# RWKV-7 time mix in a two-block network, one Trainium2 core: the next head pair's inputs one step later in VectorE's order and in smaller pieces, the inverse's first level ahead of the values' product, two result matrices behind that level

## The chip, the cores and the metric

The kernel runs on one core of one Trainium2 chip. The metric is the device time of one execution in microseconds (us). Three executions of the kernel before the change took 4197.87, 4207.27 and 4209.8 us; their median is 4207.27.

## What is computed

Two transformer-like blocks of two layers each, on a sequence of 512 positions with width 1024, all in float32. The change touches only one part of the second block's layers, the RWKV-7 time mix, which therefore runs twice in an execution. Cut to what matters, for 8 heads of 64 channels:

```python
z = z + (z_prev - z) * mu                    # token shift, per channel
r, k, v, lw, la, lg = split(z)
decay = exp(-exp(-0.5) * sigmoid(w0 + tanh(lw) @ w_up))
a = sigmoid(a0 + la @ a_up);  g = sigmoid(lg) @ g_up
kk = k * k_k;  kk = kk * rsqrt(max(sum(kk * kk), 1e-24))   # per head
kf = k * (1 + (a - 1) * k_a)
def step(state, r_t, w_t, k_t, v_t, ka_t, kb_t):           # ka = -kk, kb = kk * a
    sa = state @ ka_t
    state = state * w_t + outer(sa, kb_t) + outer(v_t, k_t)
    return state, state @ r_t
y = scan(step)                               # over 512 positions
yn = (y - mean) * rsqrt(var + eps) * ln_w + ln_b
out = (yn + sum(r * kf * r_k) * v) * g
```

## The kernel before

**The chunked form.** The recurrence isn't walked position by position. The 512 positions are cut into 8 chunks of 64. Within a chunk, products of 64x64 matrices (called grams here) of the decayed tensors `at`, `bt`, `kt`, `rt` give AT (the matrix to be inverted) and TM (its transpose), AK, RB and RK. The inverse of the triangular matrix is built by five doubling levels (`lv` 1 to 5). Each level is a product X on TensorE, its eviction to XS by ScalarE, a product T on TensorE, and the addition of T into the inverse (`T2`, `TTM`) by VectorE. W1 is the product of AK and the values. After the levels come MN (the inverse times `at` and W1), DP and E (the chunk's state update), a chain of six small products S1 to S6 (the state through the chunks, each step TensorE then VectorE), and the outputs Y and YS.

**Pairs.** Heads are taken two at a time, four pairs `pp` = 0 to 3 in each of the two time mixes. For each pair, `back(pp)` is the chunk algebra above, and `front(pp)` makes the pair's inputs: the projections k, r and v (each 24 matmuls of 512 columns in four quarters, line 2556), the decay, the normalised key, and from them `at`, `bt`, `kt`; and the bonus and gate (`bon`, `g`). The product `sq` (line 2578) sums the key's squares within a head, `bon` (line 2587) sums r*kf*r_k.

**The order.** Every engine runs its own instruction list in program order. In each list the function `interleaved` runs `front(0)` alone, and then alternates, one step at a time, `back(pp)` and `front(pp + 1)`; a step is what stands between two `yield`s. So the place of a `yield` decides behind which piece of `back` a piece of the next pair's `front` stands. Beside `back(3)` TensorE does matmuls of the following gate stage (line 3029) in place of a front. An instruction whose data aren't there yet holds up all that stands behind it on its engine.

**Engines of the pieces.** On VectorE: line 2802 adds the shifted token (for k, r, v), 2812 and 2816 are the decay's scan, 2830 is kf, 2833 evicts `sq`, 2836 is kk, 2841 is `at`, 2842 and 2845 make `bt`, 2848 is the factor for `bon`, 2849 is `kt`, 2857 and 2859 finish bonus and gate. Of back, 2864 masks the grams, 2870 and 2874 make the inverse's start, 2872 is `rt`, 2888 adds T of levels 1 to 4, 2891 that of level 5, 2894 evicts half of MN, 2899, 2902 and 2905 take DP and E, 2910 is a step of the state's chain. `vector_finish` (2515 to 2526) is the normalisation of the pair before. On GpSimd: 2930 squares the key, 2941 and 2943 prepare the levels' masks (`OFF`, one instruction a level), and `gpsimd_feed` (1481) splits a 128x1024 half of the weights into a high and a low part, after `scalar_feed` (ScalarE, 1467) has made the high part. On ScalarE: 2709 evicts a projection, 2745 and 2747 are the logarithm and exponential that make the inverse root of `sq`, 2777 evicts X.

**PSUM.** Banks 6 and 7 belong to front. Banks 0 to 5 go round for back's products in the order of the list `BACK`; a product waits until the earlier user of its bank has been evicted.

## Time and profile before

| | us |
|---|---|
| median of three executions | 4207.27 |
| lowest, highest | 4197.87, 4209.8 |
| the profiled execution, its time | 4199.9 |
| the profiled execution, its span | 4198.1 |
| first time mix, from the first gram of pair 0 (2165.3) to YS of pair 3 (2423.8) | 258.5 |
| distance between the first grams of pairs 1 and 2 | 66.2 |

The span is the time between the first and last instruction that the trace shows; the execution's own time is 1.8 us more. TensorE is busy for 94% of the span. The work of the two time mixes is alike: each has four pairs of some 64 to 66 us, with its own prologue (front of pair 0) ahead.

### The profile page before, as it was taken

What the parts mean: (1) busy time and instruction counts of PE and PEld (TensorE: products, weight loads), DVE (VectorE), ACT (ScalarE), POOL (GpSimd) and SP (SyncE); (2) the same over time, 40 slices, a digit from 0 to 9 for tenths busy, and PEclk for the clock granted to TensorE, in tenths of its full rate; (3) what the DMA queues carried; (4) which work ended last, traced back from release to release, by engine and by line L of the source; (5) the groups of instructions that cost most, each with busy time, mean ns of one, the idle gap of its engine ahead of it and who ended that gap; (6) DMA issues with size and microseconds to landing.
All of it is one profiled execution on the core that took longest, in us unless ns stands there. A gap on an engine that the chain in (4) does not pass through costs nothing.

```text
span 4198.1 us, 60801 instructions
## 1 busy us (share of the span) xinstructions
PE 3932.4 (94%) x25980; PEld 3121.3 (74%) x25980; DVE 1771.6 (42%) x2671; ACT 1435.1 (34%) x2275; POOL 1190.3 (28%) x725
## 2 busy tenths in 40 slices
PE   7988899999989899999988899999999889999998
PEld 6966678888777678877666787788776667877886
DVE  3266232323254633435845422334368454224333
ACT  3256222222244633332432333333324332333332
POOL 2010122222211033332332235333323322353332
PEclk9999999999999999999999999999999999999999
DMA  5014133323111022222111022222211100222221
GB/s 206 31 58 151 51 116 106 111 93 101 67 61 43 31 83 96 100 71 76 51 36 37 22 86 95 83 99 97 85 66 51 41 27 32 91 90 82 99 94 67
DMA packets 61358, 323.55 MB, mean 77 GB/s; under 512 B 6177, under 2 KB 6305, under 8 KB 36257
## 3 DMA queue, kind: packets, MB, share of 16 engines
q1 hardware_dynamic: 61088, 319.65, 22.1%
q8 instruction: 207, 3.39, 0.3%
q14 instruction: 63, 0.51, 0.0%
HBM read 317.53 MB, written 2.10 MB: 76 GB/s over the span
## 4 chain that ended last, share of the span: by engine, by line
PE 80%; DVE 6%; issue 5%; ACT 3%; POOL 3%; DMA 2%; SPq 0%; DVEq 0%; POOLq 0%; ACTq 0%
PE ps L1509 50%; PE ps L704 3%; PE ps L724 3%; PE ps L2556 3%; PE ps L1521 2%; PE ps L338 2%; PE ps L2192 1%; DMA adab<-in_wada 1%; PE ps L3029 1%; PE ps L1008 1%; PE ps L1043 1%; PE ps L2635 1%; PE ps L1023 1%; PE ps L2180 1%; PE ps L2648 1%
## 5 line engine op out<-in xcount | busy, mean ns | idle before, releaser
L1883 DVE SCALAR_TENSOR_TENSOR ftmp<-ps,vec,ftmp 128x511 f32<-128x511 f32 (+2 forms) x440 | 301.6, 694 | 357.4 <-ACT ftmp L1837 236.2
L1481 POOL TENSOR_TENSOR PWL<-ring,PWH 128x1024 fp32r<-128x1024 f32 (+2 forms) x116 | 266.7, 2299 | 609.6 <-ACT PWH L1467 609.6
L1481 POOL TENSOR_TENSOR WL<-ring,WH 128x1024 fp32r<-128x1024 f32 (+3 forms) x102 | 227.0, 2226 | 618.4 <-ACT WH L1467 601.9
L1467 ACT ACTIVATE PWH<-ring 128x1024 fp32r<-128x1024 f32 (+2 forms) x216 | 211.8, 982 | 480.3 <-PE ps L1509 446.1
L1467 ACT ACTIVATE WH<-ring 128x1024 fp32r<-128x1024 f32 (+3 forms) x160 | 158.7, 993 | 627.4 <-PE ps L1509 590.7
L1509 PE MATMUL ps<-FH,WH 128*128 128x512 f32 x1008 | 311.4, 363 | 0.0
L1509 PE MATMUL ps<-FH,WL 128*128 128x512 f32 x1008 | 305.6, 358 | 0.0
L1509 PE MATMUL ps<-FL,WH 128*128 128x512 f32 x1008 | 304.3, 356 | 0.0
L1481 POOL TENSOR_TENSOR PW3L<-ring,PW3H 128x1024 fp32r<-128x1024 f32 (+2 forms) x92 | 210.5, 2288 | 278.1 <-ACT PW3H L1467 277.8
L1474 DVE TENSOR_TENSOR PWL<-ring,PWH 128x1024 fp32r<-128x1024 f32 (+2 forms) x100 | 125.5, 1257 | 357.4 <-ACT PWH L1467 357.4
L1509 PEld LDWEIGHTS ps<-FH,WH 128*128 128x128 f32 x1008 | 167.8, 190 | 37.2 <-issue 9.1
L1906 POOL TENSOR_TENSOR ftmp<-ftmp 128x512 f32<-128x512 f32 (+1 forms) x88 | 126.0, 1432 | 231.9 <-DVE ftmp L1883 231.7
L1509 PEld LDWEIGHTS ps<-FL,WH 128*128 128x128 f32 x1008 | 167.4, 189 | 29.8
L1509 PEld LDWEIGHTS ps<-FH,WL 128*128 128x128 f32 x1008 | 167.1, 189 | 29.8
L1467 ACT ACTIVATE PW3H<-ring 128x1024 fp32r<-128x1024 f32 (+2 forms) x106 | 104.2, 983 | 248.4 <-PE ps L1509 237.1
L1509 PE MATMUL ps<-FH,PWL 128*128 128x512 f32 x432 | 170.9, 396 | 0.0
L1509 PE MATMUL ps<-FL,PWH 128*128 128x512 f32 x432 | 170.5, 395 | 0.0
L1509 PE MATMUL ps<-AH,WH 128*128 128x512 f32 (+1 forms) x528 | 164.5, 366 | 6.2 <-DVE AL L1888 6.2
L1509 PE MATMUL ps<-FH,PWH 128*128 128x512 f32 x432 | 169.6, 393 | 0.0
L1474 DVE TENSOR_TENSOR WL<-ring,WH 128x1024 fp32r<-128x1024 f32 (+3 forms) x58 | 67.1, 1157 | 235.2 <-ACT WH L1467 235.1
L1509 PE MATMUL ps<-AH,WL 128*128 128x512 f32 (+1 forms) x528 | 160.4, 358 | 0.0
L1509 PE MATMUL ps<-AL,WH 128*128 128x512 f32 (+1 forms) x528 | 159.6, 357 | 0.0
(599 smaller groups left out, 9805.8 us busy)
## 6 DMA issues: line engine op xcount, KB each, us to landing
ring<-in_wup SPq DMA_DIRECT2D x88, 1024.0 KB, 4.8
adab<-in_wada SPq DMA_DIRECT2D x56, 512.0 KB, 5.5
ring<-in_wgate SPq DMA_DIRECT2D x24, 1024.0 KB, 4.9
ring<-in_wdown SPq DMA_DIRECT2D x24, 896.0 KB, 4.7
ring<-in_win SPq DMA_DIRECT2D x18, 1024.0 KB, 4.8
ring<-in_wout SPq DMA_DIRECT2D x16, 1024.0 KB, 4.9
ring<-in_wada SPq DMA_DIRECT2D x14, 1024.0 KB, 5.2
ring<-in_wdown SPq DMA_DIRECT2D x12, 1024.0 KB, 5.0
```

The costliest lines, as they stand in the source:

```text
L338: e.matmul(bank(6 + i)[:, 0:n], C("ones"), buf(k * len(segs) + i)[:, 0:n], start=k == 0, stop=k == 7).then_inc(*sum_mm.up(tag, k, i))
L704: mm = e.matmul(pr[:, c:c + n], ww[:, k, :], h[part][:, k, :], start=k == 0 and x == 0, stop=k == 7 and x == 2)
L724: mm = e.matmul(out, x, ww[:, k, :], start=kk == 0 and n == 0, stop=kk == 7 and n == 2)
L1008: mm = e.matmul(two(a)[:, n:n + d_ - c], PF[r, BASE[kq] + jt, qc:qc + 128], PF[r, BASE[kk] + jt, c:d_], start=True, stop=True)
L1467: e.activation(wh, view, ACT.Copy).then_inc(*whi_a.up(L, n))
L1474: e.tensor_tensor(wl, view, wh.bitcast(F32), SUB).then_inc(*wlo_v.up(L, n))
L1481: e.tensor_tensor(wl, view, wh.bitcast(F32), SUB).then_inc(*wlo_g.up(L, n))
L1509: mm = e.matmul(out[:, c:c + h.shape[1]], ww[:, k, :], h, start=at == 0 and p == 0, stop=at == K - 1 and p == 2)
L1521: mm = e.matmul(outs[j][:, c:c + h.shape[1]], ww[:, k, :], h, start=k == order[0] and ww is ws[j][0] and part == 0, stop=k == order[-1] an ...
L1883: e.scalar_tensor_tensor(out=dst, in0=src, scalar=conv_cols(L, ch, a), in1=dst, op0=MUL, op1=ADD).then_inc(*(ffn_v.up(L, "tap", x, j, c) i ...
L1906: e.tensor_tensor(zg, zg, zv, MUL).then_inc(*ffn_g.up(L, x))
L2556: mm = e.matmul(front_bank(what), ww[:, k, :], h, start=k == 0 and x == 0, stop=k == 7 and x == 2)
```

## The change

It does four things; all are moves, and no arithmetic instruction is added or removed.

- On VectorE all of the next pair's front stands one step later or more, so behind the levels' additions where it stood ahead of them: the decay's scan behind T1's addition, K behind T3's, and, above all, R, kk, `at`, `bt` behind T5's. The piece that held R, kk, `at` and `bt` is cut into R; kk and `at`; and bon's factor with `bt`. ScalarE's order is fitted to it (R is evicted ahead of the logarithm).
- On TensorE the products `sq`, `bon` and `g` come one step or more later.
- At the head of back, X of level 1 comes ahead of W1, and the grams RB and RK move from ahead of them to behind T of level 1, with their masks on VectorE. `rt` is made after AK's mask. The order of PSUM banks follows.
- On GpSimd the k weights' split comes ahead of the squares of the key.

```diff
-        BACK = ([... for x in ("AT", "TM", "tok0", "tok1", "tok2", "tok3", "AK", "RB", "RK", "W1")] ...
+        BACK = ([("AT", 2), ("TM", 2)] + [(f"tok{i}", 1) for i in range(4)] + [("AK", 2)] + level(1, "X") + [("W1", 1), ("mean", 1)] + level(1, "T")
+                + [("RB", 2), ("RK", 2)] + level(2, "X") + [("var", 1)] + level(2, "T") + [y for lv in range(3, 6) for x in "XT" for y in level(lv, x)]
...
 tensor front
                     quarter(q, pp, "r")
-                    if q == 1:
+                    if q == 2:
                         w.wait_ge(rw_v.at(L, pp, "K"), rw_g.at(L, pp, "sq"))
                         e.matmul(front_bank("sq"), ...)
...
                     quarter(q, pp, "v")
-                    if q == 2:
-                        w.wait_ge(rw_v.at(L, pp, "R"), rw_v.at(L, pp, "bon"))
-                        e.matmul(front_bank("bon"), ...)
                     if q < 3:
                         yield 1
+                yield 1
+                w.wait_ge(rw_v.at(L, pp, "R"), rw_v.at(L, pp, "bon"))
+                e.matmul(front_bank("bon"), ...)
                 yield 1
                 w.wait_ge(rw_v.at(L, pp, "V"), rw_a.at(L, "sig"))
                 e.matmul(front_bank("g"), ...)
...
 tensor back
                 gram("AK", kt, at, kt_)
-                gram("RB", bt, rt, rt_)
-                gram("RK", kt, rt)
                 yield 1
-                (the W1 product)
                 for lv in range(1, 6):
                     (the X product of both halves)
+                    if lv == 1:
+                        (the W1 product)
                     next(fin, None)
                     yield 1
                     (the T product of both halves)
+                    if lv == 1:
+                        gram("RB", bt, rt, rt_)
+                        gram("RK", kt, rt)
                     yield 1
...
 vector front
+                yield 1
                 w.wait_ge(rw_a.at(L, pp, "lw"))
                 (scan, lp, u, K, KN, kf)
                 yield 1
+                yield 1
                 w.wait_ge(rw_mm.at(L, pp, "sq"))
                 e.tensor_scalar(TSQ, front_bank("sq"), ...)
                 yield 1
+                shifted((L, pp, "R"), R, front_bank("r"), pp)
+                yield 1
                 w.wait_ge(rw_a.at(L, pp, "isq"))
                 e.tensor_tensor(KN, KN, TSQ, MUL)
-                yield 1
-                shifted((L, pp, "R"), R, front_bank("r"), pp)
                 (at)
+                yield 1
+                (bon's factor)
                 (b, bt)
                 yield 1
-                (bon's factor)
                 e.tensor_tensor(kt, KF, TGI, MUL)
-                yield 1
-                yield 1
                 yield 1
                 shifted((L, pp, "V"), VV, front_bank("v"), 8 + pp)
                 yield 1
                 (bonus)
+                yield 1
                 (gate)
...
 vector back
-                w.wait_ge(rw_a.at(L, pp, "GT"))
-                e.tensor_tensor(rt, R, GT, MUL)
                 mine(L, pp, "TTM0")
                 e.tensor_tensor(TTM, TTM, many("id2"), ADD)
                 masked("AK", AKT, "su")
-                masked("RB", RBT, "iu")
-                masked("RK", RKT, "iu")
+                w.wait_ge(rw_a.at(L, pp, "GT"))
+                e.tensor_tensor(rt, R, GT, MUL)
...
                     (T additions of level lv)
+                    if lv == 1:
+                        masked("RB", RBT, "iu")
+                        masked("RK", RKT, "iu")
...
 gpsimd front
+                gpsimd_feed(e, w, F, pair_view(pp + 1, "k"))
                 w.wait_ge(rw_v.at(L, pp, "KN"), ...)
                 e.tensor_tensor(TSQ, KN, KN, MUL)
-                gpsimd_feed(e, w, F, pair_view(pp + 1, "k"))
```

In the diff, what stands in brackets or as "..." within a line is unchanged code told in a word. All tensors of this part are cells of one tile `ar`; so the rows that follow are told apart by their lines.

VectorE before, from T4's additions (2888) of pair 1 to the masks of DP: kk (2836), R (2802), `at` (2841), `bt` (2842, 2845), and only then T5's additions (2891), bon's factor (2848), `kt` (2849), MN's eviction (2894).

```order
L2888 TENSOR_TENSOR ar<-ar,ps 128x2x256 x2
L2836 TENSOR_TENSOR ar<-ar,HC 128x512
L2802 SCALAR_TENSOR_TENSOR ar<-ps,vec,ar 128x511
L2841 SCALAR_TENSOR_TENSOR ar<-ar,HC 128x512
L2842 TENSOR_TENSOR ar<-ar 128x512
L2845 TENSOR_TENSOR ar<-ar,HC 128x512
L2891 TENSOR_TENSOR ar<-ar,ps 128x256 x2
L2848 SCALAR_TENSOR_TENSOR ar<-ar,vec 128x512
L2849 TENSOR_TENSOR ar<-ar,HC 128x512
L2894 COPY ar<-ps 128x4x2x64
L2899 TENSOR_TENSOR ar<-ps,cst 128x512
```

The same place on VectorE after the change (its own line numbers: 2892 is T4, 2839 the eviction of `sq`, 2895 T5, 2806 R, 2901 MN, 2844 kk, 2847 `at`, 2906, 2909 and 2912 DP and E, 2850 bon's factor, 2851 and 2854 `bt`).

```order
L2839 TENSOR_SCALAR HC<-ps 128x512
L2895 TENSOR_TENSOR ar<-ar,ps 128x256 x2
L2806 SCALAR_TENSOR_TENSOR ar<-ps,vec,ar 128x511
L2901 COPY ar<-ps 128x4x2x64
L2844 TENSOR_TENSOR ar<-ar,HC 128x512
L2847 SCALAR_TENSOR_TENSOR ar<-ar,HC 128x512
L2906 TENSOR_TENSOR ar<-ps,cst 128x512
L2909 TENSOR_TENSOR ar<-ps,ar 128x512
L2912 TENSOR_TENSOR ar<-ar,ps 128x512
L2850 SCALAR_TENSOR_TENSOR ar<-ar,vec 128x512
L2851 TENSOR_TENSOR ar<-ar 128x512
L2854 TENSOR_TENSOR ar<-ar,HC 128x512
```

What stood ahead of T5's additions stands behind them; kk and `at` now lie between MN's eviction and DP's, and bon's factor and `bt` ahead of the first step of the state's chain (2917), which is the next row.

TensorE before, at the head of pair 1: AT and TM (the first 2605), the transposes, AK with RB and RK (the second 2605, 48 matmuls), W1 (2625), X1 (2635), the mean of the pair before.

```order
L2605 MATMUL ps<-ar 64x64 x32
L2615 MATMUL ps<-cst,ar 128x128 x16
L2605 MATMUL ps<-ar 64x64 x48
L2625 MATMUL ps<-ar 64x64 x16
L2635 MATMUL ps<-ar 64x64 x16
L2494 MATMUL ps<-XC,cst 128x512
```

The same place after the change: the second group of grams (2606) is AK alone, 2628 is X1, 2636 is W1.

```order
L2606 MATMUL ps<-ar 64x64 x32
L2616 MATMUL ps<-cst,ar 128x128 x16
L2606 MATMUL ps<-ar 64x64 x16
L2628 MATMUL ps<-ar 64x64 x16
L2636 MATMUL ps<-ar 64x64 x16
L2495 MATMUL ps<-XC,cst 128x512
```

The 32 matmuls of RB and RK stand behind T1 now, ahead of the first quarter of the next k.

## Rows read from the trace of the kernel before

**Rows 1.** The page's first part: span, and busy time of each engine.

```profile
span 4198.1 us, 60801 instructions
...
PE 3932.4 (94%) x25980; PEld 3121.3 (74%) x25980; DVE 1771.6 (42%) x2671; ACT 1435.1 (34%) x2275; POOL 1190.3 (28%) x725
```

**Rows 2.** Waits of TensorE, first time mix (2130 to 2460): us, times, longest.

```profile
PE ps L2658 <- DVE ar L2891: 11.1, 3, 3.7
```

**Rows 3.** The same view of the second time mix (3280 to 3600).

```profile
PE ps L2658 <- DVE ar L2891: 11.2, 3, 3.7
```

**Rows 4.** The same view of pair 1, its first row left out.

```profile
PE ps L2682 <- DVE ar L2910: 1.5, 3, 0.7
PE ps L2592 <- DVE ar L2802: 1.3, 1, 1.3
PE ps L2625 <- DVE ar L2864: 1.0, 1, 1.0
PE ps L2635 <- DVE ar L2888: 1.0, 1, 1.0
PE ps L2605 <- DVE ar L2872: 0.6, 1, 0.6
PE ps L2556 <- ACT HC L2727: 0.4, 1, 0.4
```

**Rows 5.** Timeline of VectorE in pair 1: start, duration, instruction, idle before.

```profile
2258.40 2.89 DVE L2830 TENSOR_TENSOR ar<-ar,XC 128x512 f32<-128x512 f32 x1
...
2270.68 2.84 DVE L2842 TENSOR_TENSOR ar<-ar 128x512 f32<-128x512 f32 x1
...
2274.16 0.75 DVE L2891 TENSOR_TENSOR ar<-ar,ps 128x256 f32<-128x256 f32 x2
2274.83 0.75 DVE L2848 SCALAR_TENSOR_TENSOR ar<-ar,vec 128x512 f32<-128x512 f32 x1
...
2278.56 0.69 DVE L2894 COPY ar<-ps 128x512 f32<-128x512 f32 x1 [2.39 <-PE ps L2658]
...
2284.99 0.28 DVE L2910 SCALAR_TENSOR_TENSOR ar<-ps,ar 128x64 f32<-128x64 f32 x1 [1.45 <-PE ps L2682]
```

**Rows 6.** Timeline of GpSimd in pair 1.

```profile
2258.37 2.37 POOL L1481 TENSOR_TENSOR PWL<-ring,PWH 128x1024 fp32r<-128x1024 f32 x1
2270.41 2.56 POOL L1481 TENSOR_TENSOR PW3L<-ring,PW3H 128x1024 fp32r<-128x1024 f32 x1 [9.67 <-ACT PW3H L1467]
```

**Rows 7.** Timeline of TensorE: MN to Y's start, pair 1, then MN, pair 3.

```profile
2275.06 3.47 PE L2658 MATMUL ps<-ar 64*64 64x128 f32 x32 [3.71 <-DVE ar L2891]
2278.45 0.50 PE L2556 MATMUL ps<-PXH,PWH 128*128 128x512 f32 x1
...
2291.81 0.49 PE L2691 MATMUL ps<-ar 64*64 64x64 f32 x7
...
2403.38 1.96 PE L2658 MATMUL ps<-ar 64*64 64x128 f32 x32
2405.28 0.51 PE L3029 MATMUL ps<-PXH,PWH 128*128 128x512 f32 x1
```

**Rows 8.** Busy times over pair 1's MN; 0.60 is TensorE's granted clock.

```profile
2275.00:2279.00 4.00, 3.94 (x34) 3.74 (x35) 1.61 (x3) 0.44 (x1) 0.00 (x0) 0.60 0.55 229
```

**Rows 9.** Timeline of VectorE, head of pair 1: masks of AK, RB, RK.

```profile
2235.37 1.87 DVE L2864 TENSOR_TENSOR ar<-ps,cst 128x512 f32<-128x512 f32 x3
```

**Rows 10.** Line 2943 in 2229 to 2242: nanoseconds of one, least, median and most.

```profile
L2943 POOL TENSOR_TENSOR ar<-ar,cst x5: 1271/1286/1742, 2233.2 to 2239.0; 128x512 f32<-128x512 f32 x5
```

**Rows 11.** Timeline of TensorE: W1 in pair 1, then W1 in pair 2.

```profile
2236.10 1.15 PE L2625 MATMUL ps<-ar 64*64 64x64 f32 x32 [1.04 <-DVE ar L2864]
...
2301.88 1.84 PE L2625 MATMUL ps<-ar 64*64 64x64 f32 x32 [1.04 <-DVE ar L2864]
```

**Rows 12.** Timeline of TensorE in the first prologue: `sq` and `bon`.

```profile
2148.22 1.10 PE L2578 MATMUL ps<-HC,cst 128*128 128x512 f32 x2 [0.93 <-POOL HC L2930]
...
2158.53 1.88 PE L2587 MATMUL ps<-ar,cst 128*128 128x512 f32 x2 [2.30 <-DVE ar L2848]
```

More of the change, by code:

```diff
@@ L2432, in program, with level @@
         FRONT_BANK = {"w": 6, "a": 7, "k": 6, "r": 7, "sq": 6, "bon": 7, "v": 6, "g": 6}
-        BACK = ([(x, 1 if x[0:3] == "tok" or x == "W1" else 2) for x in ("AT", "TM", "tok0", "tok1", "tok2", "tok3", "AK", "RB", "RK", "W1")]
-                + [((x, lv, h), 1) for lv in range(1, 6) for x in ("X", "T") for h in range(2)]
+        def level(lv, x):
+            return [((x, lv, h), 1) for h in range(2)]
+        BACK = ([("AT", 2), ("TM", 2)] + [(f"tok{i}", 1) for i in range(4)] + [("AK", 2)] + level(1, "X") + [("W1", 1), ("mean", 1)] + level(1, "T")
+                + [("RB", 2), ("RK", 2)] + level(2, "X") + [("var", 1)] + level(2, "T") + [y for lv in range(3, 6) for x in "XT" for y in level(lv, x)]
                 + [("MN", 2), ("DP", 2), ("E", 2)] + [(("S", c), 1) for c in range(1, 7)] + [("Y", 2), ("YS", 1)])
-        at_lv = BACK.index((("X", 1, 1), 1)) + 1
-        BACK = BACK[:at_lv] + [("mean", 1)] + BACK[at_lv:at_lv + 4] + [("var", 1)] + BACK[at_lv + 4:]
         def back_banks():
@@ L2584, in front @@
                     quarter(q, pp, "v")
-                    if q == 2:
-                        w.wait_ge(rw_v.at(L, pp, "R"), rw_v.at(L, pp, "bon"))
-                        e.matmul(front_bank("bon"), C("b64"), BON[pp % 2], start=True, stop=True).then_inc(*rw_mm.up(L, pp, "bon"))
                     if q < 3:
                         yield 1
+                yield 1
+                w.wait_ge(rw_v.at(L, pp, "R"), rw_v.at(L, pp, "bon"))
+                e.matmul(front_bank("bon"), C("b64"), BON[pp % 2], start=True, stop=True).then_inc(*rw_mm.up(L, pp, "bon"))
                 yield 1
@@ L2617, in back @@
                 gram("AK", kt, at, kt_)
-                gram("RB", bt, rt, rt_)
-                gram("RK", kt, rt)
                 yield 1
-                pr = back_ps("W1")
-                w.wait_ge(*back_free(L, pp, "W1"), rw_v.at(L, pp, "AK"), rw_a.at(L, pp, "tok3"))
-                for t, hh, s in UNITS:
-                    z = 2 * t + hh
-                    mm = e.matmul(pr[rows(s), z * 64:z * 64 + 64], AKT[rows(s), z, :], vtk[rows(s), z, :], start=True, stop=True)
-                mm.then_inc(*rw_mm.up(L, pp, "W1"))
                 fin = tensor_finish(e, w, L, pp - 1) if pp else iter(())
@@ L2637, in back @@
                         mm.then_inc(*rw_mm.up(L, pp, "X", lv, h))
+                    if lv == 1:
+                        pr = back_ps("W1")
+                        w.wait_ge(*back_free(L, pp, "W1"), rw_v.at(L, pp, "AK"), rw_a.at(L, pp, "tok3"))
+                        for t, hh, s in UNITS:
+                            z = 2 * t + hh
+                            mm = e.matmul(pr[rows(s), z * 64:z * 64 + 64], AKT[rows(s), z, :], vtk[rows(s), z, :], start=True, stop=True)
+                        mm.then_inc(*rw_mm.up(L, pp, "W1"))
                     next(fin, None)
@@ L2841, in front @@
                 e.scalar_tensor_tensor(out=at, in0=KN, scalar=-1.0, in1=TLP, op0=MUL, op1=MUL).then_inc(*rw_v.up(L, pp, "at"))
+                yield 1
+                mine(L, pp, "R")
+                e.scalar_tensor_tensor(out=BON[pp % 2], in0=R, scalar=vc("rw_r_k_2", 4 * l + pp), in1=KF, op0=MUL, op1=MUL).then_inc(*rw_v.up(L, pp, "bon"))
                 e.tensor_tensor(bt, KN, AA, MUL).then_inc(*rw_v.up(L, pp, "b"))
@@ L2846, in front @@
                 yield 1
-                mine(L, pp, "R")
-                e.scalar_tensor_tensor(out=BON[pp % 2], in0=R, scalar=vc("rw_r_k_2", 4 * l + pp), in1=KF, op0=MUL, op1=MUL).then_inc(*rw_v.up(L, pp, "bon"))
                 e.tensor_tensor(kt, KF, TGI, MUL).then_inc(*rw_v.up(L, pp, "kt"))
-                yield 1
-                yield 1
                 yield 1
```

16 lines of the change are left out of this document (9 added, 7 removed).

## The prediction

> **What bounds the kernel now.** The page comes first: TensorE is busy for 3932.4 of 4198.1 us [rows 1], so only what makes TensorE wait, or work slowly, can move the time, and all four edits lie inside the two time mixes. The next view is therefore who TensorE waits for there. One cause stands far above the rest: MN (2658) waits for T5's additions (2891), three times 3.7 us in each mix, 11.1 and 11.2 us [rows 2, 3]. It is three times and not four because pair 3 has no front beside it. The same view of one pair lists what else is left: 1.3 us ahead of `g`, 1.5 us in the state's chain, 1.0 ahead of W1, 1.0 ahead of X2, 0.6 ahead of RB, 0.4 ahead of k [rows 4]; with MN's 3.7, some 9.5 of a pair's 66.2 us.
>
> Why are T5's additions late? VectorE's timeline answers. `bt`'s first product (2842) stands ahead of them and takes 2.84 us [rows 5], where other instructions of its size take 0.69 [rows 5]. It starts 0.27 us after GpSimd's split of weights, 2270.41 to 2272.97 [rows 6], and ends 0.55 us after it, so it stood still until GpSimd was through. T5's additions start at 2274.16 and TensorE goes on at 2275.06, having stood since 2271.35 [rows 5, 7].
>
> The wait has a second price. MN's 32 matmuls take 3.47 us behind the wait and 1.96 in pair 3, where none is [rows 7]; the granted clock over them is 0.60 [rows 8], so that part of the time ran at the lower level, 1.2 GHz. From MN's start to that of the next matmul it is 3.39 against 1.90 us [rows 7]: 1.49 us a pair.
>
> The Trainium skill ("SBUF — State Buffer", Who interferes with whom) says that a VectorE instruction with two SBUF inputs contends with a GpSimd instruction that reads SBUF, the later one waiting the other out. By that rule, the trace agrees (2.84 against 0.69 us).
>
> **The parts and their costs.** I walk each pair in the new order with the durations of the old trace.
>
> *T5 first.* In the new order only the eviction of `sq`, a 0.69 us instruction whose product is done a step earlier, stands between T4's and T5's additions. T5's products end about when the first quarter of v starts, so the two additions (0.75 us together) are over before that quarter (1.7 us) is. MN's wait goes: 3.71 x 3 = 11.1 us a mix. With no wait the clock has no cause to fall there: 1.49 x 3 = 4.5 us. Bounds for the clock: nothing (it falls anyway) to 1.49.
>
> *The late stretch on VectorE.* What left T5's front goes where TensorE is in MN to S6. From MN's end VectorE must do: N 0.69, kk and `at` 1.4, DT, E and P 2.1, bon's factor and `bt` 2.1, S1 0.28, `kt` 0.7, S2, V 0.75, S3, bonus 0.7, S4, gate 0.7, S5, S6: 11 us, of which each large one costs about 0.7 and each step of the chain 0.28 [rows 5]. TensorE took 13.4 us from the quarter behind MN, 2278.45, to Y, 2291.81 [rows 7], 2.8 of them in waits [rows 4], so it has 10.6 us of work there and the two are nearly level. Walking it: E is evicted 4.5 us after MN's end, P, bon's factor and `bt` last until 7.0, S1's eviction until 7.3, so S2 waits 0.3 us; bon fills S3's wait and `g` finds V just ready; S5 waits 0.5 (behind the gate's eviction), S6 0.6. Sum 1.4 us, against 1.3 + 1.5 = 2.8 before [rows 4]: a gain of 1.4 x 3 = 4.3 us a mix. This is where the change adds waits: bon's factor and `bt` now have S1's eviction and with it the chain queued behind them, and kk (which waits for ScalarE's root, now behind R's eviction and a 1.05 us split) has DT, E and P behind it. ScalarE is done some 1.7 us before kk's turn. GpSimd's split of the r weights ended at 2272.97 [rows 6]; 1.4 us sooner (the head's gain, below) that is 2271.6. MN can start at 2271.35 less 1.4, ends 1.96 later and N takes 0.69 [rows 5, 7], so kk starts at 2272.6, about 1 us behind the split's end, and neither it nor `bt` should meet one. If one does, it costs 2.84 - 0.69 = 2.2 us [rows 5], bound from below by nothing.
>
> *The head.* X1 no longer waits for W1, and W1 no longer for RB and RK's masks queue, but X1 needs the first of GpSimd's level masks, which starts at 2233.2 and takes 1.74 us [rows 10]: X1 can start at 2234.9. AK ended about 2233.3: W1's start, 2236.10, less its wait of 1.04, RB's and RK's 32 matmuls (1.15, as W1's [rows 11]) and the 0.6 ahead of them [rows 4]. So one wait of about 1.65 us takes the place of 0.6 and 1.0: nothing gained. T1's additions now stand ahead of the scan and of RB's and RK's masks (0.62 each [rows 9]); k's first quarter and X2 find everything ready: the 0.4 and 1.0 go [rows 4]. Gain 1.4 us in pairs 1 and 2, 0.3 to 0.5 in pair 0 (it has no such wait for ScalarE), nothing in pair 3, whose waits are those at the start of the head alone: 3.1 us a mix.
>
> *K, kf and the normalisation.* kf takes 2.89 us now, beside GpSimd [rows 5, 6]. In the new order it stands behind the normalisation's two products, and those meet the split and the squares instead. I let each wait its turn: the three are over just as T4's first half is due, with 1 us to spare at least before X5 needs it. Cost nothing; the cover is X4, the quarter of r and T4.
>
> *The GpSimd swap.* `sq`'s input is made 2.4 us later [rows 6], but its product stands a quarter and a level later. Nothing in a pair.
>
> *The prologue.* Front of pair 0 runs alone, so there order is all. `sq` waits for GpSimd 0.93 us now [rows 12]; with the split ahead about 1.9. `bon` waits 2.30 now and makes the next quarter slow [rows 12]; then it stands behind the last quarter of v and waits about 0.6. `g` comes when V is ready. My walk puts the first gram 3 us earlier, or 1 us later if `kt` meets a split or the clock falls behind `sq`: 2 us a mix, bounds -1 and +3.
>
> Sum a mix: 11.1 + 4.5 + 4.3 + 3.1 + 2.0 = 25.0; two mixes 50 us. Against the profiled execution's 4199.9 that gives 4150. The median of the three runs is 7.4 us above that execution, so a median of the changed kernel should lie at 4157; I take **4156**.
>
> **The rivals.**
>
> *The late stretch gives part of it back.* VectorE's 11 us against TensorE's 10.6 leave no room. If kk or `at`, or `b`, meets GpSimd's split, the chain starts 2.2 us later in each of six pairs, 13 us, and a clock that falls behind the longer waits takes up to 1.5 more in each, 9 us. Then the gain is 28 to 37 us: about 4174. For it: MN comes 3.7 us sooner, the split does not, so the distance between them shrinks to 1 us. Against it: that 1 us is still there by the rows. The Trainium skill's rule above, on two SBUF inputs, would put `at` and bon's factor under it too, which are of another kind of instruction. No row here shows one of those beside a split from its start.
>
> *The wait ahead of MN only shrinks.* Something else is late when T5's additions aren't, `sq` or ScalarE's eviction of X5; then half of 3.7 stays and the clock falls still: the gain is 4.3 + 3.1 + 2 + 5.5 = 15 us a mix or less, 30 in all or less, down to 12 if the chain loses what the head gains: 4177 to 4195. In the rows X5's eviction and `sq` are both over microseconds before, so I give it little.
>
> *No net change.* What was idle in front of MN appears in the chain as waits of VectorE: the same work, another place. It takes 8 us of new waits a pair, and the walk finds 1.4.
>
> *Slower.* The one long wait of 1.65 us at the head could let the clock fall. It does fall there already in some pairs: W1 took 1.15 us in pair 1 and 1.84 in pair 2, behind the same wait [rows 11]. At the lower level a stretch takes up to double. The gain of some 8 us a pair is eaten once more than 8 us of full-speed work run slowly in each; if the head stays slow until T2 is through, 15 us of work, a pair loses 7 us, the eight pairs lose 55, and the time is about 4260. Against it: the fall seen lasts for W1 and X1 alone.
>
> **Chances.** Forecast (gain of 38 to 60): 0.62. Late stretch gives back (25 to 38): 0.20. Wait only shrinks (12 to 25): 0.08. No net change: 0.06. Slower: 0.04. A measurement of this kernel tells about 0.3%, 12.6 us, from no change. So faster 0.90, same 0.06, slower 0.04. The range: the upper side of the forecast, with the clock holding in the chain too and the prologue at its best, is a gain of 62, 4144 with the spread of the runs 4142; the other side goes through the second case and into the third, 4186. The likeliest one's own range is 4142 to 4169.
>
> **What would show it right or wrong.** In the view of waits, MN's row (3.7 us, three a mix) is gone; MN's 32 matmuls take near 2 us with a clock near 1 in pairs 0 to 2. X1's first wait is for GpSimd's line of level masks, about 1.6 us; X2's wait is gone. In the chain, small waits for VectorE that sum to 1 to 2 us a pair. The distance from pair 1's first gram to pair 2's falls from 66.2 to about 58. On VectorE, `b` takes 0.7 us. It is wrong if a 2.8 us kk or `b` shows between MN and S1, if MN still waits, or if TensorE's work at the lower clock grows.

## The result, and the profile after

The changed kernel takes 4130.88 us (median of four executions, 4129.3 to 4139.48) against 4205.85 us for the kernel before on the same chip (four executions, 4197.87 to 4209.8). The ratio is 0.9828, with a 95% interval from 0.9808 to 0.9848: 64 to 81 us faster. The prediction said 4156, with a range that ended at 4142; the gain is larger than it allowed.

The page of the changed kernel, its span and busy times, against [rows 1]:

```profile
span 4127.7 us, 60817 instructions
...
PE 3900.0 (94%) x25980; PEld 3095.7 (75%) x25980; DVE 1749.5 (42%) x2671; ACT 1433.2 (35%) x2275; POOL 1191.6 (29%) x725
```

TensorE runs the same 25980 matmuls in 32.4 us less busy time: part of the gain isn't waits, but work that ran slowly before, some of it outside the time mixes (below). The span is 70.4 us shorter, so the other 38 are idle time. Who TensorE waits for in the first mix (2130 to 2460; us, times, longest), against [rows 2, 4]:

```profile
PE ps L2628 <- POOL ar L2950: 6.9, 4, 2.0
PE ps L2685 <- DVE ar L2917: 2.5, 6, 0.5
PE ps L2557 <- ACT HC L2730: 2.0, 1, 2.0
PE ps L2579 <- POOL HC L2938: 1.7, 1, 1.7
PE ps L2593 <- DVE ar L2806: 1.4, 1, 1.4
```

and in the second mix (3250 to 3600), against [rows 3]:

```profile
PE ps L2628 <- POOL ar L2950: 7.3, 4, 2.0
PE ps L2685 <- DVE ar L2917: 2.5, 6, 0.5
```

MN's row is gone. X of level 1 (2628) waits for GpSimd's level masks four times, 1.8 us on average. The state's chain (2685) waits 0.8 us a pair. Each of the three rows below those stands once, in the prologue. TensorE's timeline in pair 1, against [rows 7, 11]; first X1 and W1, then MN and the quarter behind it, then the end of the chain and the next pair's first gram:

```profile
2220.63 1.97 PE L2628 MATMUL ps<-ar 64*64 64x64 f32 x32 [1.14 <-POOL ar L2950]
2222.34 1.91 PE L2636 MATMUL ps<-ar 64*64 64x64 f32 x32
...
2256.70 1.96 PE L2661 MATMUL ps<-ar 64*64 64x128 f32 x32
2258.59 0.50 PE L2557 MATMUL ps<-PXH,PWH 128*128 128x512 f32 x1
...
2269.28 0.33 PE L2685 MATMUL ps<-ar 64*64 64x64 f32 x4 [0.39 <-DVE ar L2917]
2270.07 0.33 PE L2685 MATMUL ps<-ar 64*64 64x64 f32 x4 [0.46 <-DVE ar L2917]
...
2271.93 0.27 PE L2606 MATMUL ps<-ar 64*64 64x64 f32 x2
```

MN starts without a wait and takes 1.96 us for 3.47. From S6 to the next pair's first gram, the stretch of Y and YS, it is 2271.93 - 2270.07 = 1.86 us. In the kernel before these two rows of the timeline stand 3.13 us apart:

```profile
2291.64 0.35 PE L2682 MATMUL ps<-ar 64*64 64x64 f32 x4 [0.39 <-DVE ar L2910]
...
2294.77 0.37 PE L2605 MATMUL ps<-ar 64*64 64x64 f32 x2
```

The busy times over these stretches say why (the number behind GpSimd's is TensorE's granted clock). The end of pair 1's chain, in the kernel before:

```profile
2293.00:2295.00 2.00, 2.00 (x63) 2.00 (x61) 0.69 (x1) 0.00 (x0) 0.00 (x0) 0.50 0.95 397
```

and in the changed kernel X1 and W1, and the end of the chain:

```profile
2219.00:2225.00 6.00, 4.86 (x94) 4.17 (x88) 1.86 (x3) 1.36 (x3) 6.00 (x5) 0.72 0.01 3
...
2270.00:2272.50 2.50, 2.43 (x129) 2.43 (x133) 1.15 (x4) 0.00 (x0) 0.00 (x0) 1.00 0.52 141
```

Before, the engine was at the lower level, 1.2 GHz, at the chain's end; now it is at 2.4 GHz there, as in MN, whose 32 matmuls take the 1.96 us that pair 3's took before [rows 7, 8]; over X1 and W1 it falls in part (0.72 in that stretch). VectorE's timeline in pair 1, against [rows 5] (kk, `at`, and later `b`):

```profile
2259.32 0.68 DVE L2844 TENSOR_TENSOR ar<-ar,HC 128x512 f32<-128x512 f32 x1
2260.03 0.69 DVE L2847 SCALAR_TENSOR_TENSOR ar<-ar,HC 128x512 f32<-128x512 f32 x1
...
2264.26 0.69 DVE L2851 TENSOR_TENSOR ar<-ar 128x512 f32<-128x512 f32 x1
```

GpSimd's split, which held `b` up before [rows 6], is over at 2258.22, 1.1 us before kk:

```profile
2255.85 2.37 POOL L1481 TENSOR_TENSOR PW3L<-ring,PW3H 128x1024 fp32r<-128x1024 f32 x1 [9.16 <-ACT PW3H L1467]
```

**Where the time came from.** I cut each pair at five starts on TensorE: the first gram, X2, MN, the matmul behind MN, and the last group of S6. "Head" is first gram to X2, "levels" X2 to MN, "MN" to the matmul behind it, "chain" from there to S6, and "end" from S6 to the next pair's first gram (in pair 3 to the last YS). The prologue runs from the mix's first projection matmul (w, a or k's) to pair 0's first gram. Sums over the pairs, in us (the gain is that of the two mixes together, and the predicted one is twice the prediction's term for a mix):

```
            mix 1 before  after    mix 2 before  after   both mixes: gained  predicted
prologue          32.29   30.34          32.66   30.26              4.4        4.0
head              65.54   60.99          63.94   61.79              6.7        6.2
levels           114.47  102.99         114.52  103.00             23.0       22.2
MN                11.38    7.58          11.90    7.57              8.1        9.0
chain             54.98   48.99          55.76   48.99             12.8        8.6
end               12.16    9.54          13.04    9.55              6.1        0
sum              290.82  260.43         291.82  261.16             61.1       50.0
```

Levels, MN, chain and end of pairs 0 to 2 now take the same in both mixes to 0.03 us (pair 1: 25.86, 1.89, 11.48, 1.86), where before the end took anything from 2.48 to 3.26. From pair 1's first gram to pair 2's it is now 57.1 us, for 66.2 (I had said about 58). The two mixes explain 61.1 of the 70.4 us between the two traces. TensorE's waits in them sum to 75.4 us before and 34.6 after, so 41 of the 61 us are waits and 20 are work that ran slowly. The other 9.3 us lie in parts that the change doesn't touch: 2.7 ahead of the first mix and 6.7 behind the second, with 0.1 the other way between them. The first experiment asks what they are.

### The profile page after: what moved, and what is told of

The parts are those of the page before. It is cut to its first block, busy times and chain, and to the rows that moved or that the text cites. A ratio compares the mean times of both kernels' runs of the same rounds, so it can differ in the third digit from the quotient of the medians.

```text
span 4127.7 us, 60817 instructions
## 1 busy us (share of the span) xinstructions
PE 3900.0 (94%) x25980; PEld 3095.7 (75%) x25980; DVE 1749.5 (42%) x2671; ACT 1433.2 (35%) x2275; POOL 1191.6 (29%) x725
## 4 chain that ended last, share of the span: by engine, by line
PE 82%; DVE 5%; issue 5%; POOL 4%; ACT 3%; DMA 2%; SPq 0%; DVEq 0%; POOLq 0%; ACTq 0%
PE ps L1509 51%; PE ps L704 3%; PE ps L724 3%; PE ps L2557 3%; PE ps L1521 2%; PE ps L338 2%; DMA adab<-in_wada 1%; PE ps L3036 1%; PE ps L1008 1%; PE ps L2192 1%; PE ps L1043 1%; PE ps L2628 1%; PE ps L2650 1%; PE ps L2648 1%; PE ps L1023 1%
```

## The experiments

All marks below are those of the table. The kernels named first to fourth ran on one chip, beside 13 executions of the kernel before (median 4199.11, 4192.84 to 4212.39).

**The kernel before, once more.** No edit.

> The kernel before, unchanged, profiled once more. In the first trace the matmuls of the last feed-forward part (behind the second time mix) stand 0.2333 us apart, in the changed kernel's trace 0.2289, which makes 6.7 us of difference in a part that the change does not touch. If that is a matter of the single execution, this trace shows 0.2289 there and a part of some 627.6 us behind the second mix; if it belongs to the kernel before (where its data or code lie), it shows 0.2333 and 634 us again. The two time mixes should take 258.4 and 259.0 us from first gram to last YS, as before.

4201.27 us in one execution. Its mixes are 291.49 and 293.58 us, 585.1 against the first trace's 582.6; behind the second mix it has 629.3 us, where the first trace had 634.1: neither of the two values that I had named. So the part behind the mixes isn't a property of the kernel. What differs there is TensorE's pace, at full granted clock, in stretches with no wait. Busy times over two stretches of the kernel before, first trace (the count in brackets is that of the matmuls in 100 us):

```profile
1700.00:1800.00 100.00, 100.00 (x438) 82.06 (x437) 42.80 (x56) 34.88 (x45) 36.16 (x19) 1.00 0.30 100
...
3900.00:4000.00 100.00, 100.00 (x431) 80.98 (x430) 30.67 (x39) 30.37 (x38) 34.62 (x17) 1.00 0.28 95
```

and the last stretch in the changed kernel's first trace:

```profile
3900.00:4000.00 100.00, 100.00 (x439) 82.05 (x438) 34.20 (x45) 33.13 (x45) 38.19 (x20) 1.00 0.28 91
```

Between 431 and 439 matmuls lie 2%, in one trace from stretch to stretch as well as between traces. The mixes of the kernel before differ by 2.4 us between its two traces, 0.4 of it waits and the rest slow clock: so MN and chain of pair 1 of the second mix take 3.61 and 14.60 us for 3.29 and 13.19.

**The head alone.** The changed kernel with the old fronts on every engine: what is left of the change is the order of X1, W1, RB and RK, their banks, and `rt`.

```diff
 tensor front, of the changed kernel
-                    if q == 2:
+                    if q == 1:
                         w.wait_ge(rw_v.at(L, pp, "K"), rw_g.at(L, pp, "sq"))
                         e.matmul(front_bank("sq"), ...)
...
 vector front
-                yield 1
                 w.wait_ge(rw_a.at(L, pp, "lw"))
...
(R, kk, at, bon's factor, b, bt, ScalarE's root and GpSimd's split as in the kernel before)
```

> Only the edits of back: X1 ahead of W1, RB and RK behind T1, rt and the banks, with the fronts of before. My theory (the gain is the front's move): MN waits 3.7 us in each of six pairs as before, T1's additions stand behind the scan as before, so X2 waits about 1 us; k's 0.4 us wait goes; gain 0 to 5 us in all, the time within 0.3% of before. The rival (the head is worth its part of the change, freeing the start of each pair): 12 us or more, two a pair over six.

4192.08 us (4184.12 to 4202.53, ten executions), ratio 0.9978 (0.9966 to 0.999). The mixes are 287.50 and 286.27, together 11.3 us shorter than those of the kernel before in the same group (7 us by the medians): more than I gave it. MN still waits 3.7 us. In mix 1 the head gains 3.7 us (60.11 against 63.85), all else together 0.3. In mix 2 the head gains only 0.5, but MN's stretch gains 2.2 and the end 4.1 (9.55 against 13.66). X1 and W1 of pair 1 in mix 1, then X1 and W1 of pair 1 in mix 2, TensorE's timeline:

```profile
2243.69 1.15 PE L2628 MATMUL ps<-ar 64*64 64x64 f32 x32 [1.77 <-POOL ar L2948]
2244.65 1.13 PE L2636 MATMUL ps<-ar 64*64 64x64 f32 x32
...
3378.55 1.63 PE L2628 MATMUL ps<-ar 64*64 64x64 f32 x32 [1.97 <-POOL ar L2948]
3379.91 1.98 PE L2636 MATMUL ps<-ar 64*64 64x64 f32 x32
```

The same program has its slow stretch in two different places: where Y and YS are slow (3.26, 2.53 and 2.40 us in mix 1) X1 and W1 are quick, and where Y and YS are quick (1.86 in all three pairs of mix 2) X1 or W1 is slow. In those three pairs of mix 2 the chain has the same waits as in the kernel before (1.3 us ahead of `g`, then 0.71, 0.39 and 0.39), and what follows it still runs at full clock: the waits alone don't decide it.

**The fronts alone.** The kernel before with the new fronts on every engine, and the old head.

```diff
 vector front, of the kernel before
+                yield 1
                 w.wait_ge(rw_a.at(L, pp, "lw"))
...
+                shifted((L, pp, "R"), R, front_bank("r"), pp)
+                yield 1
                 w.wait_ge(rw_a.at(L, pp, "isq"))
                 e.tensor_tensor(KN, KN, TSQ, MUL)
-                yield 1
-                shifted((L, pp, "R"), R, front_bank("r"), pp)
...
(tensor, scalar and gpsimd front as in the changed kernel)
```

> Only the fronts' edits, on all four engines, with back and the banks of before. My theory: nearly all of the gain, MN's wait and its slow clock gone, the chain as in the changed kernel, X2's 1 us wait gone too since the scan is behind T1's additions; what is missing is k's 0.4 us. Gain in the two mixes 56 to 62 us of the 61.2 of the full change. The rival (front and head need each other, since RB's and RK's masks and rt now stand ahead of the later pieces): 45 us or less.

4133.85 us (4128.81 to 4135.6), ratio 0.9848 (0.9831 to 0.9864). The mixes are 259.34 and 258.77, together 518.1: 64.5 us less than the first trace of the kernel before, where I had expected 56 to 62, and 3.5 us less than with the whole change. The whole executions can't tell the two versions apart. Levels, MN, chain and end are those of the changed kernel to 0.1 us in sum. The head is shorter than there, 60.37 and 59.40 against 60.99 and 61.79. So the gain of the head is there with the fronts alone, and beside them the new order of X1 takes some of it back, though beside the old fronts it gained. About half of the head's 9.7 us in this kernel is X2's wait for T1's additions, 4.8 us in the two mixes, which is gone because the scan stands behind them. The 3.0 us that the new order costs are the clock: TensorE's waits in the heads come to 15.8 us here and to 15.6 in the changed kernel; W1 and X1 of pair 2, TensorE's timeline, in this kernel:

```profile
2275.91 1.15 PE L2625 MATMUL ps<-ar 64*64 64x64 f32 x32 [0.78 <-DVE ar L2866]
2276.89 1.10 PE L2635 MATMUL ps<-ar 64*64 64x64 f32 x32
```

In the changed kernel X1 and W1 of pair 1 take 1.97 and 1.91 us behind a wait of 1.14 and one of 0.50 just ahead of it. X1 or W1 is slow there in pairs 1 and 2 of both mixes, in all three traces of that kernel; with the old head it is in pair 3 of the first mix alone. But pairs 0 and 3 of the changed kernel have the same kind of wait and keep the clock; pair 3 of the first mix:

```profile
2335.12 1.15 PE L2628 MATMUL ps<-ar 64*64 64x64 f32 x32 [1.97 <-POOL ar L2950]
2336.07 1.13 PE L2636 MATMUL ps<-ar 64*64 64x64 f32 x32
```

So the slow stretch comes with the new order, but the length of X1's wait doesn't say in which pair.

**T5's additions first, and nothing else.** Two lines of the kernel before.

```diff
                 e.tensor_tensor(KN, KN, TSQ, MUL).then_inc(*rw_v.up(L, pp, "kk"))
                 yield 1
+                yield 1
                 shifted((L, pp, "R"), R, front_bank("r"), pp)
...
                 e.tensor_tensor(kt, KF, TGI, MUL).then_inc(*rw_v.up(L, pp, "kt"))
                 yield 1
                 yield 1
-                yield 1
                 shifted((L, pp, "V"), VV, front_bank("v"), 8 + pp)
```

> The kernel before with one yield moved: R, at, b and bt stand one step later on VectorE, behind T5's additions; nothing else is changed. By the terms of the prediction MN's wait (3.7 us) and its slow clock (1.5 us) go in six pairs: 31 us, less 0.1 us a pair for DP behind a late N. The clock over Y, YS and the next AT stays at the lower level as before, since bon and g aren't in the chain: S6 to the next first gram 3.1 us, not the 1.9 of the changed kernel. So a gain of 28 to 31 us. The rival (this one move is the whole gain, and the rest of the edits are level): 45 us or more, with the clock up behind the chain.

4167.27 us (4165.68 to 4174.8), ratio 0.9929 (0.9915 to 0.9944). The mixes are 276.90 and 275.04, together 30.7 us shorter than the first trace's, as expected. All of it lies at MN: levels 22.7 (103.15 in each mix), MN 8.1 (7.57 and 7.59). Chain and end gain nothing (the chain loses 2.1 us, the head gains 2.2): four of the six ends between pairs take 2.84 us or more, and none less than 2.49. So half of the mixes' gain is that one reordering, and MN's wait isn't what makes the chain's end slow. From this kernel to the changed one, 30.4 us, chain and end gain 21.4, head and prologue 8.7. A row of VectorE in this kernel settles what the prediction left open, `at` beside GpSimd's split, with `b` behind it:

```profile
2271.21 2.54 DVE L2842 SCALAR_TENSOR_TENSOR ar<-ar,HC 128x512 f32<-128x512 f32 x1
2273.67 0.68 DVE L2843 TENSOR_TENSOR ar<-ar 128x512 f32<-128x512 f32 x1
```

while GpSimd's timeline has

```profile
2270.84 2.36 POOL L1481 TENSOR_TENSOR PW3L<-ring,PW3H 128x1024 fp32r<-128x1024 f32 x1 [9.66 <-ACT PW3H L1467]
```

The split holds `at` up too, until 2273.75, 0.55 us behind the split's end: 2.54 us for 0.69. MN's eviction on VectorE stands behind it, so DP now waits 0.58 us in each of the six pairs, where I had expected 0.1. The Trainium skill ("SBUF — State Buffer", Who interferes with whom) says it of any VectorE instruction with two SBUF inputs. By that rule `at` should be blocked, and the trace agrees.

The next four ran together on a second chip, beside seven executions of the kernel before (median 4198.79, 4194.38 to 4206.02).

**The changed kernel, once more.** No edit.

> The changed kernel once more, as the measure on the same chip for the three beside it: 0.982 of before, the two mixes 260.4 and 261.2 us from the first projection product to the last YS, S6 to the next first gram 1.86 us, MN 1.96 us.

4141.65 us (4136.8 to 4153.99), ratio 0.9868 (0.9848 to 0.9887): 11 us above the first median, and the ratio's interval leaves out the 0.982 that I had expected. The profiled execution is the slowest, 4153.99, and yet its mixes are 260.38 and 260.67, together 521.1, as in the first trace. It spends 2148.5 us ahead of the first mix and 634.0 behind the second (2130.3 and 627.4 in the first). Its pace at the end is the lower one:

```profile
3900.00:4000.00 100.00, 100.00 (x430) 81.00 (x429) 35.55 (x46) 35.19 (x47) 36.70 (x19) 1.00 0.27 90
```

So between executions of the changed kernel the parts outside the mixes differ by up to 25 us, and the mixes by less than 1 (those of the kernel before by 2.4, above).

**The pieces not cut.** kk, `at`, bon's factor, `b` and `bt` in one piece.

```diff
                 e.scalar_tensor_tensor(out=at, in0=KN, scalar=-1.0, in1=TLP, ...)
-                yield 1
                 (bon's factor, b, bt)
                 yield 1
+                yield 1
                 e.tensor_tensor(kt, KF, TGI, MUL).then_inc(*rw_v.up(L, pp, "kt"))
```

> The changed kernel with kk, at, bon's factor and bt in one piece again, between N and DT on VectorE, in place of two. By my walk DT starts 2 us later but is not waited for; E's eviction ends 0.9 us later, S1 waits 0.25 us, and S2 comes when it does now. So the cut is worth 0 to 2 us in all: the same time as the changed kernel within 3 us. The rival (the smaller pieces are what keeps the chain short): 2 us a pair, 12 us slower or more.

4141.14 us (4140.48 to 4146.16), ratio 0.9864 (0.985 to 0.9879); mixes 521.6. That cut is worth nothing here.

**`bon` and `g` back to their old places.** The changed kernel with the two products between the chain's steps moved a step forward again.

```diff
                     quarter(q, pp, "v")
+                    if q == 2:
+                        w.wait_ge(rw_v.at(L, pp, "R"), rw_v.at(L, pp, "bon"))
+                        e.matmul(front_bank("bon"), ...)
                     if q < 3:
                         yield 1
                 yield 1
-                w.wait_ge(rw_v.at(L, pp, "R"), rw_v.at(L, pp, "bon"))
-                e.matmul(front_bank("bon"), ...)
-                yield 1
                 w.wait_ge(rw_v.at(L, pp, "V"), rw_a.at(L, "sig"))
                 e.matmul(front_bank("g"), ...)
```

> The changed kernel with bon's product beside the third quarter of v and g's behind S2 again, as before. It asks what the clock at the end of the chain hangs on. bon then waits 0.6 us for its factor, g 1.4 us for V, S4 to S6 0.4 each with nothing between: 2.1 us more waits a pair than the changed kernel. If the denser chain is what kept the clock up (theory), S6 to the next first gram goes from 1.86 back to about 3.1 us: together 3.4 us a pair, 20 us slower in all. If the clock hung on MN's wait alone (rival), that distance stays 1.86 and the loss is 12 us.

4162.28 us (4159.79 to 4164.71), ratio 0.991 (0.9894 to 0.9927). The mixes are 541.6, 20.0 us longer than with the change, as expected. The chain loses 13.6 of them (55.81 and 55.77 for 48.99 and 48.99), the end 7.6 (13.38 and 13.29 for 9.54 and 9.55), the prologue 2.0, and the head gets 3.1 back. Who waits in the first mix:

```profile
PE ps L2593 <- DVE ar L2806: 5.5, 4, 1.6
PE ps L2685 <- DVE ar L2917: 3.8, 9, 0.5
PE ps L2588 <- DVE ar L2850: 3.4, 4, 2.1
```

and the busy times over the end of pair 1's chain, where the granted clock is 0.64:

```profile
2289.00:2293.00 4.00, 3.14 (x87) 3.00 (x89) 1.83 (x6) 0.00 (x0) 0.43 (x1) 0.64 0.60 199
```

Two things happen. `g` waits 1.3 us for V again, `bon` 0.4, and the chain has three waits a pair and not two: 6.5 us more in a mix's pairs than in the changed kernel (each row less its wait in the prologue, where `g` waits 1.56 and `bon` 2.08), 13.0 in both, which is the chain's loss but for 0.6. And the end, where TensorE waits for nothing, is slow again: 2.83 to 3.26 us for 1.86. With `bon` and `g` between S2, S3 and S4 the clock holds: in the nine traces of kernels that have them there, all 54 ends between pairs take 1.86 us. In the five that don't, 27 of 30 take 2.40 to 3.26; the three others are those of the head-only kernel's second mix.

**The level masks sooner.** X1's wait is what is left in every pair, also in pair 3. GpSimd makes TM with the identity added (2948, 1.66 us) ahead of the first level mask. In this kernel VectorE adds it, and GpSimd starts with the masks.

```diff
 vector back
                 masked("TM", TM, "l0")
+                mine(L, pp, "TM")
+                e.tensor_tensor(TM, TM, many("id2"), ADD).then_inc(*rw_v.up(L, pp, "TMI"))
+                masked("AK", AKT, "su")
                 (TTM)
-                masked("AK", AKT, "su")
...
 gpsimd back
-                w.wait_ge(rw_v.at(L, pp, "TM"))
-                e.tensor_tensor(TM, TM, many("id2"), ADD).then_inc(*rw_g.up(L, pp, "TM"))
+                w.wait_ge(rw_v.at(L, pp, "AT"))
```

> The changed kernel with the identity added to TM by VectorE right behind TM's mask, AK's mask ahead of TTM, and GpSimd starting with the level masks. X1's wait of 2.0 us for GpSimd is the longest left in a pair, and in some pairs X1 and W1 run slowly behind it. If the first level mask and TM are ready by AK's end, the wait goes in eight pairs, 16 us, and with it some slow clock, 1 us in most of them: 15 to 24 us faster than the changed kernel. The rival (VectorE's additions and GpSimd's masks hold each other up, so T1 waits for TTM instead): less than 6 us.

4119.79 us (4118.08 to 4133.89), ratio 0.9818 (0.98 to 0.9837). The mixes are 252.14 and 253.26, 16.2 us shorter than with the change, all of it in the head (53.09 and 53.82 for 60.99 and 61.79) but for 0.4. X1's wait for GpSimd is gone from the view (one pair keeps 0.8 us that the view puts down to no engine), and X1 and W1 run at full clock. In pair 1 of the first mix, but for X1's first matmul:

```profile
2218.56 1.15 PE L2628 MATMUL ps<-ar 64*64 64x64 f32 x31
2219.61 1.15 PE L2636 MATMUL ps<-ar 64*64 64x64 f32 x32
```

The rest ran on two further chips. **GpSimd's swap undone.**

```diff
-                gpsimd_feed(e, w, F, pair_view(pp + 1, "k"))
                 w.wait_ge(rw_v.at(L, pp, "KN"), ...)
                 e.tensor_tensor(TSQ, KN, KN, MUL).then_inc(*rw_g.up(L, pp, "sq"))
+                gpsimd_feed(e, w, F, pair_view(pp + 1, "k"))
```

> The changed kernel with GpSimd's square of the key ahead of the k weights' split again, as before. By my walk sq is not waited for in a pair either way; only the prologues see it: TensorE waits 0.9 us ahead of sq in place of 1.7. So the two mixes together are 0 to 2 us shorter than the changed kernel's 521.6, which a whole execution can't show, its other parts differing by 10 us and more. The rival (kf then meets the split, T4's additions come late, X5 waits): 1 us a pair, 6 us longer.

4136.36 us in one execution, which says nothing by itself, but its mixes are 257.12 and 257.97: 6.5 us shorter than with the change, where I expected next to nothing. The prologue takes 27.74 and 27.84 us for 30.34 and 30.26, and pair 0's head 13.23 and 13.22 for 13.92. TensorE's timeline in the prologue, `sq`, `bon`, `g` and the first grams, here

```profile
2152.98 1.02 PE L2579 MATMUL ps<-HC,cst 128*128 128x512 f32 x2
...
2164.15 1.13 PE L2593 MATMUL ps<-cst,small 128*128 128x512 f32 x2 [1.41 <-DVE ar L2806]
2165.20 1.16 PE L2606 MATMUL ps<-ar 64*64 64x64 f32 x64
```

and in the changed kernel, against [rows 12]:

```profile
2147.67 1.10 PE L2579 MATMUL ps<-HC,cst 128*128 128x512 f32 x2 [1.73 <-POOL HC L2938]
...
2156.40 1.10 PE L2590 MATMUL ps<-ar,cst 128*128 128x512 f32 x2 [0.65 <-DVE ar L2850]
...
2158.90 1.80 PE L2593 MATMUL ps<-cst,small 128*128 128x512 f32 x2 [1.40 <-DVE ar L2806]
2160.64 1.99 PE L2606 MATMUL ps<-ar 64*64 64x64 f32 x64
```

`sq`'s wait of 1.73 is gone, and with the same wait of 1.4 us ahead of `g`, `g` and the grams run at full clock, 0.67 and 0.83 us quicker: 3.2 of some 3.3 us a mix. Only the 1.73 are sure to be `sq`'s: in the first mix of the fronts-only kernel and of the one with the level masks sooner `sq` waits the same 1.73 us, and `g` (1.13) and the first grams (1.16) run at full clock all the same.

**The square a step later.** In the kernel with the masks sooner, ScalarE's square of the normalisation (`next(fin)`) stood ahead of k's first quarter, which waited for it 1.7 us in one pair, 0.9 and 0.8 in two others, and not in the fourth.

```diff
-                    next(fin, None)
                     yield 1
+                    next(fin, None)
                     yield 1
```

> The kernel e7 with one more yield moved: on ScalarE the square of the normalisation stands behind the next pair's two sigmoids, not ahead of them. In e7 TensorE waits 1.7 us ahead of k's first quarter, which needs the decay's sigmoid out of its bank, and this stands behind a table load and the square, which waits for the mean. With the square behind, k waits for nothing in pairs 1 and 2: 1.7 us in each of four, 6 to 7 us less than e7's 505.4 us in the two mixes. The rival (the square is late for the variance's product, and that wait takes its place): within 2 us of e7.

4119.13 us (4116.08 to 4130.16, five executions), ratio 0.98 (0.9778 to 0.9821; 4204.5 for nine of the kernel before). The mixes are 501.0, 4.4 us shorter than without the edit; I expected 6 to 7, having taken the 1.7 us for all four pairs; the quarter's waits summed to 3.4, and they are gone. The 4.4 aren't all theirs: the second mix is 5.0 us shorter and the first 0.6 longer, and the prologues, which the edit doesn't touch, hold 1.3. By the whole executions the two kernels are the same.

**All three.** The masks sooner, the square later and GpSimd's swap undone (the three diffs above together).

> The kernel e8 with the square of the key ahead of the split again on GpSimd. In e6 that alone took 2.6 us off each prologue and 0.7 off each pair 0, with no wait ahead of sq and no slow clock at the first gram. If the three are independent the two mixes take 501.0 - 6.6 = 494 us, 27 us less than the changed kernel's. If the swap's gain rests on the head of the changed kernel (whose first level waits for GpSimd anyway), it is less than 2 us here.

> The changed kernel a third time, on the same chip as e9, so that the two are compared in the same rounds: 521 us in the two mixes, 0.984 of before.

4110.19 us (4102.1 to 4117.08, five executions), ratio 0.9773 (0.9759 to 0.9787), beside 4205.77 (nine executions, 4200.81 to 4209.49) of the kernel before. The changed kernel, beside it on the same chip, has a median of 4138.37 in five executions, one of which took 14131.74 us for a reason that nothing here shows (the other four 4125.88 to 4142.15), and a ratio, without that one, of 0.9836 (0.9821 to 0.9851). So this is the quickest version, 28 us ahead of the change by the medians. Its mixes are 248.56 and 247.30, together 495.9 against 521.4. I had expected 494: the swap undone gives 5.1 us here, for 6.5 alone. The longest row of waits left in its first mix is the chain's:

```profile
PE ps L2685 <- DVE ar L2919: 2.5, 6, 0.5
```

## Why the prediction was wrong

**What held.** The bound and the mechanism. MN's wait went whole: levels gained 23.0 us for 22.2, and the two-line experiment shows that T5's additions alone do it. MN's clock came back with it, 8.1 for 9.0. X1 waits 1.1 to 2.0 us for GpSimd (I said 1.65), X2 no longer, and W1 has no wait. `b` takes 0.69. The split ends 1.1 us before kk (I said about 1), so the rival in which the late stretch gives back didn't come; `at` beside the split in the two-line experiment shows that its price of about 2 us was real. The prologue gained 4.4 for 4.0, with waits of 1.73 for `sq` and 0.65 for `bon` where I said 1.9 and 0.6.

**How far off.** The forecast was 4156, the median is 4131. Of these 25 us the mixes hold 11 (a gain of 61 for 50); the other 14 lie outside them or in the base, and are told below.

**The step that failed: the late chain.** I counted its waits and gave its clock nothing in the sum; only the upper end of the range ("with the clock holding in the chain too") had it. The sum had "4.3" a mix for the late chain; chain and end together gained 8.6 and 10.3, 18.9 in both mixes for 8.6. Two things were mis-sized. The waits left are 0.4 at S5 and 0.5 at S6, 0.85 a pair and not 1.4: S2's isn't there. Six pairs by 0.55 are 3.3 us. The rest, 7 us, is clock: Y and YS, 6.1 us, and chain matmuls that ran slowly in some pairs before. The row that showed it was in the trace of before, at 2293 to 2295 with a clock of 0.50, directly behind pair 1's last row in [rows 7]. I had looked at the clock at MN and at W1, not behind the chain. The experiment that puts `bon` and `g` back shows what brought it: with nothing else changed, chain and end lose 21.2 us, 13.0 of them as waits and 7.6 in the end, where there is no wait at all. It isn't MN's wait: with T5 first and the old chain the ends stay slow (2.49 to 3.26 us).

**The head was right in sum and wrong in parts.** It gained 6.7 for 6.2. Its waits gained 4.9 us, the rest is clock. The fronts alone give 9.7, and the new order of X1, W1, RB and RK then costs 3.0 there (3.5 with the prologue, one trace against three that agree to 0.6). This is the slower rival's mechanism in small: behind X1's wait W1 and X1 take up to 2.01 and 1.97 us for 1.15, in pairs 1 and 2. In pairs 0 and 3 they don't, behind waits of up to 1.97 us. It ended where "against it" said, behind those two, and never cost the pair more than some 1.6 us.

**The swap on GpSimd was priced at nothing in a pair, and rightly, but the prologue paid for it.** I put `sq`'s longer wait into the walk; a clock that falls behind it was only in the bound ("or 1 us later"), and the slow `g` and first grams are that case. Without the swap the mixes are 6.5 us shorter (one execution, both mixes together), 3.4 of them `sq`'s wait.

**The base.** By the mixes the gain is 61 us, just inside the "gain of 62" at which the range ended, and 4205.85 less 61 is 4145, which the range holds. The median lies 14 us below that. In the profiled execution 9.3 us of the difference lie outside the mixes, where nothing was edited and executions of one kernel differ by more, and two later groups of the same kernel gave 4141.65 and 4138.37, with mixes of 521.1 and 521.4. The sum carried one profiled execution and 7.4 us of offset as though the rest of the kernel stood still, and its range left a share of 2 us to "the spread of the runs".

**Open.** Why the clock's slow stretch falls behind the chain in one mix of the head-only kernel and behind X1's wait in the other, why X1's wait brings it in pairs 1 and 2 and not in 0 and 3, and why `g`, 11 us behind `sq`'s wait of 1.73 us, is slow in some prologues and quick in others, isn't settled: no run varied these alone. Nor was each of the fronts' edits ahead of T5 run by itself, so beyond X2's 4.8 us the split of the head's 9.7 us among the scan, K and the normalisation is not known.

## What to carry to other kernels

When a wait is removed, ask for every stretch of small dependent matmuls behind it what its granted clock is, not only what it waits; behind a chain with waits of 0.4 to 1.3 us, 2 us of ready work ran at down to half clock here, and two independent products placed between the chain's steps gave 21 us back, 8 of them beyond the waits. Measure each part of a compound change beside the others: here the swap cost 6.5 us and the head's order, which alone had gained 11, cost 3.5 beside the new fronts, both hidden by one part that gave 31. And compare stretches between fixed marks of the trace, which agreed to 1 us with the change and to 2.4 before, ahead of comparing totals that differ by 10 to 25.

## What the runs showed of the hardware

- A VectorE `scalar_tensor_tensor` with both inputs in SBUF stood still beside a GpSimd `tensor_tensor` as a `tensor_tensor` does: 2.54 us for 0.69.
- TensorE issued 430 or 439 matmuls of 512 columns in 100 us, both at a granted clock of 1.00 and with no wait; the pace changed between stretches of one execution and between executions, of the kernel before and of the changed one alike. The part behind the mixes took 627.4 us in one trace and 634.1 in another.
- The granted clock fell to 0.50 in a stretch in which TensorE was busy all the time (Y and YS, 2.00 of 2.00 us), behind a chain with three waits of 0.4 to 0.7 us and one of 1.3; it was 1.00 in the same stretch behind two waits of 0.4 and 0.5. The waits alone don't decide it: in one mix of the head-only kernel it was 1.00 behind the first four waits too.
